# A decoder trunk on one core: one DVE step moved ahead of another at the end of each MLP chunk, and the first tile's loads and the first norm's sums rearranged

## The reference

```python
def rmsnorm(x, g):
    xf = x.astype(jnp.float32)
    y = xf * lax.rsqrt(jnp.mean(xf * xf, axis=-1, keepdims=True) + EPS)
    return (y * g.astype(jnp.float32)).astype(x.dtype)

def mlp_sq_relu(hn, w_up, w_down):
    return jnp.square(jax.nn.relu(hn @ w_up)) @ w_down

for i in range(2):
    h = h + mixer_i(rmsnorm(h, norm_mix[i]))
    h = h + mlp_sq_relu(rmsnorm(h, norm_mlp[i]), w_up[i], w_down[i])
    gate = sigmoid(rmsnorm(h, norm_ple[i]) @ w_ple_gate[i])
    h = h + gate * (p[i] @ w_ple_proj[i])
return rmsnorm(h, norm_final)
```

## Time and profile before

| what | us |
|---|---|
| median of 3 runs | 2712.83 (2710.03 to 2713.29) |
| profiled execution, its own time | 2713.6 |
| span of that execution, first to last instruction | 2712.0 |
| PE busy | 2617.7 (97%) |
| DVE, ACT, POOL busy | 1696.2, 1055.2, 812.5 |
| mean granted TensorE clock | 0.989 of full |

### The profile page before, as it was taken

The page is one execution under the profiler, slowest core; times in us unless marked ns, Lnnn a source line. Parts: engine busy times, 40 slices in busy tenths (PEclk is TensorE's granted clock), DMA queues, the critical chain, the costliest instruction groups (busy, mean ns, idle before and its releaser), DMA issues.

```text
span 2712.0 us, 33195 instructions
## 1 busy us (share of the span) xinstructions
PE 2617.7 (97%) x12228; PEld 2159.2 (80%) x12228; DVE 1696.2 (63%) x2432; ACT 1055.2 (39%) x1758; POOL 812.5 (30%) x687
## 2 busy tenths in 40 slices
PE   7999999799999999999999999989999999999996
PEld 5777888678888888888778888878888888888885
DVE  6766655544667666775664667664566766667555
ACT  5555533433333333334442324353333333333432
POOL 6000000023555555552120000002355554555213
PEclk9999999999999999999999999999999999999998
DMA  3010010031111111111231011013121111111121
GB/s 127 24 32 24 24 32 24 1 117 47 55 55 46 49 50 60 55 49 47 91 103 38 32 32 33 30 40 101 39 62 47 47 55 48 55 55 55 47 78 70
DMA packets 39387, 140.49 MB, mean 52 GB/s; under 512 B 4368, under 2 KB 4384, under 8 KB 39248
## 3 DMA queue, kind: packets, MB, share of 16 engines
q1 hardware_dynamic: 36448, 128.99, 15.4%
q0 software_dynamic: 2224, 7.54, 0.8%
q10 hardware_dynamic: 576, 2.10, 0.2%
HBM read 129.70 MB, written 8.91 MB: 51 GB/s over the span
## 4 chain that ended last, share of the span: by engine, by line
PE 74%; issue 15%; DVE 5%; ACT 4%; DMA 1%; POOL 1%; DVEq 0%; POOLq 0%; SPq 0%; ACTq 0%
PE gemm_ps L480 15%; PE gemm_ps L482 15%; PE gemm_ps L481 15%; PE s_ps L480 7%; PE s_ps L482 7%; PE s_ps L481 7%; PE to_ps L582 1%; DVE wlo L1422 1%; PE to_ps L481 1%; PE to_ps L482 1%; PE to_ps L480 1%; POOL sumsq L884 1%; ACT prob L1090 1%; DVE h L2067 0%; ACT pt_hi L1119 0%
## 5 line engine op out<-in xcount | busy, mean ns | idle before, releaser
L480 PE MATMUL gemm_ps<-b_hi,whi 128*128 128x512 f32 x1280 | 501.4, 392 | 7.8 <-DVE wlo L1422 7.8
L482 PE MATMUL gemm_ps<-b_hi,wlo 128*128 128x512 f32 x1280 | 498.2, 389 | 0.0
L481 PE MATMUL gemm_ps<-b_lo,whi 128*128 128x512 f32 x1280 | 498.2, 389 | 0.0
L480 PE MATMUL gemm_ps<-a_hi,whi 128*128 128x512 f32 x1024 | 428.5, 418 | 20.5 <-DVE a_lo L1431 12.5
L482 PE MATMUL gemm_ps<-a_hi,wlo 128*128 128x512 f32 x1024 | 405.2, 396 | 0.0
L481 PE MATMUL gemm_ps<-a_lo,whi 128*128 128x512 f32 x1024 | 404.5, 395 | 0.0
L1422 DVE TENSOR_TENSOR wlo<-wraw,whi 128x1024 fp32r<-128x1024 f32 x162 | 222.9, 1376 | 136.8 <-ACT whi L1016 136.0
L480 PE MATMUL s_ps<-hid_hi,whi 128*128 128x512 f32 x784 | 305.0, 389 | 0.0
L481 PE MATMUL s_ps<-hid_lo,whi 128*128 128x512 f32 x784 | 305.0, 389 | 0.0
L482 PE MATMUL s_ps<-hid_hi,wlo 128*128 128x512 f32 x784 | 305.0, 389 | 0.0
L480 PEld LDWEIGHTS gemm_ps<-b_hi,whi 128*128 128x128 f32 x1280 | 240.3, 188 | 64.1 <-DVE wlo L1422 13.7
(11 more groups left out here) (261 smaller groups left out, 4481.2 us busy)
## 6 DMA issues: line engine op xcount, KB each, us to landing
wraw<-panels SPq DMA_DIRECT2D x162, 512.0 KB, 3.6
wraw<-pairs SPq DMA_DIRECT2D x56, 512.0 KB, 3.6
h<-x_t SPq DMA_DIRECT2D x12, 512.0 KB, 5.5
h_spill<-h POOLq DMA_DIRECT2D x8, 512.0 KB, 3.1
h<-h_spill SPq DMA_DIRECT2D x8, 512.0 KB, 4.8
out_t<-h SPq DMA_DIRECT2D x8, 512.0 KB, 2.8
h<-x_t ACTq DMA_DIRECT2D x4, 512.0 KB, 10.6
p_raw<-p_t POOLq DMA_DIRECT2D x2, 1024.0 KB, 6.2
```

The source lines that it names most:

```text
L480: nc.tensor.matmul(out, hi_w, hi_x, start=start, stop=False, skip_group_check=True)
L481: nc.tensor.matmul(out, hi_w, lo_x, start=False, stop=False, skip_group_check=True)
L482: return nc.tensor.matmul(out, lo_w, hi_x, start=False, stop=stop, skip_group_check=True)
```

## The change

Three edits. The low part of the next up panel is made after `make_u3` and before the sixth product's read, where it stood after that read. x's tile 0 is loaded in two halves, one as SP's first load and one as ACT's first, both ahead of panel 0; ACT waits for the first half by a semaphore of its own. The first norm's squares are added by DVE, each right after the `a_lo` of its half tile, and POOL's 16 instructions for them are gone, so POOL goes to the masks straight away.

```diff
+        x_first = sem("x_first")
...
+                    sp.dma_start(h[:, 0, half_cols(1)], x_t[0, :, half_cols(1)]).then_inc(x_loaded[0], 16)
                     load_panel(Idx(0))
-                    sp.dma_start(h[:, 0], x_t[0]).then_inc(x_loaded[0], 16)
                     load_panel(Idx(1))
...
-            all_squares(0)
...
+            act.dma_start(h[:, 0, half_cols(0)], x_t[0, :, half_cols(0)]).then_inc(x_first, 16)
             for o in range(1, KT, 2):
                 act.dma_start(h[:, o], x_t[o]).then_inc(x_loaded[o], 16)
...
             for o in range(KT):
-                act.wait_ge(x_loaded[o], 16)
                 for half in range(2):
+                    act.wait_ge(x_first if (o, half) == (0, 0) else x_loaded[o], 16)
                     finish(0, Idx(o), half, a_hi)
...
-                            later = [lambda: None] * 4 + [lambda: w_lo(Idx(n + UPS + 1))] + [lambda: None] * 2
+                            later = [lambda: None] * 3 + [lambda: w_lo(Idx(n + UPS + 1))] + [lambda: None] * 3
...
                     split_lo(0, Idx(o), half, Idx(2 * o + half), a_hi, a_lo)
+                    dve.wait_ge(sq_ready, 2 * o + half + 1)
+                    if o == 0:
+                        V.tensor_copy(sumsq[:, half], zs[:, half]).then_inc(sq_added, 1)
+                    else:
+                        dve.wait_ge(sq_added, 2 * o + half - 1)
+                        V.tensor_tensor(sumsq[:, half], sumsq[:, half], zs[:, half], ALU.add).then_inc(sq_added, 1)
```

## The result

| what | before | after |
|---|---|---|
| median, us | 2712.69 (2710.03 to 2715.31, 6 runs) | 2692.12 (2691.24 to 2693.41, 6 runs) |
| profiled execution, own time | 2713.6 | 2693.33 |
| its span | 2712.0 | 2691.7 |
| granted TensorE clock, mean | 0.989 | 0.989 |

The ratio is 0.9928 (0.9916 to 0.994): 20.6 us faster. The forecast was 2697.3 with a range of 2694.0 to 2702.5. The direction and both mechanisms were right.

What follows compares the result with a forecast made beforehand. PE was taken as the bound, busy 97% of the span, so gains come from its stands or slow matmuls. Boundaries 11.5 plus start 4.8 made 16.3 us off 2713.6, giving 2697.3, range 2694.0 to 2702.5.

Steps and rivals of the forecast that it cites:

- term of 11.5: At 14 up-panel boundaries: the `wlo` moved ahead removes all of PE's 0.82 us each, 11.5 us.
- 4.8: At the start: us gained from halving tile 0's load and adding the squares on DVE, chosen from 3.7 to 5.7.
- So tile 6 ends at 33.7 to 34.7: At the start: PE's end of tile 6, from 14.2 plus 78 matmuls of 17.7 us and slow-pitch losses.
- late end: At the start: slow pitch ends when it did before, 2.8 us lost, tile 6 at 34.7, gain 4.7 us.
- fear of the masks: At the start: POOL's mask selects might hold DVE until 36.4, putting tile 7 at 37.4, a gain of only 3.7 us.
- interpolated 11.8: At the start: panel 1's landing time, interpolated from SP's earlier loads, against 13.8 before.
- early end of my own bounds, 5.7: At the start: 1.8 us lost to slow matmuls, tile 6 at 33.7, tile 7 at 35.4, gain 5.7 us.
- 1.7 us of the norm's sums: At the start, between tiles 6 and 7: the first norm's sums on PE take 1.7 us when nothing is late.
- 14.1 + 7 x 2.6: At the start: DVE handles tiles 1 to 7 from 14.1 at 2.6 us each, ending at 32.4.
- first rival: At the start: shared load engines and slow DVE leave a gain of 0 to 2 us, 2700 to 2702; chance 0.09.
- second rival: At the boundary: POOL takes the port, `wlo` ends at 721.35, 1.4 us lost over 14, total 2710; chance 0.05.
- third rival: POOL takes the port throughout: `wlo` ends at 721.7, 7 us lost, nothing won at the start, 2720.6; chance 0.02.

Runs made afterwards that it cites:

- masks_late: Changed kernel with POOL's mask building held back until DVE's sixteen additions of the first norm are done: 2692.85 us.
- start_only: Kernel before plus only the halved tile 0 loads and the first norm's sums on DVE, without the moved `wlo`: 2704.81 us against 2711.55.
- pool_ahead: Changed kernel with two memsets of dead tiles on DVE ahead of each boundary's `wlo`: 2703.23 us, 11.1 more than the changed kernel.
- boundary_only: Kernel before plus only the `wlo` moved ahead of the sixth product's read: 2699.61 us against 2711.55.
- pool_first: Changed kernel with one short memset of a dead tile on DVE ahead of each boundary's `wlo`: 2692.8 us.

## Why the prediction was right in kind and short in size

**Edit 1: right.** The waits went, the `wlo` stands right behind `make_u3` with 1.22 us and 0.7 us to spare, and POOL pays, as predicted. The term of 11.5 was a little small. From the pair's last matmul to the panel's tenth took 3.14 us before and 2.27 now, so a boundary gave 0.87 and not 0.82: a few matmuls behind a stall run at 0.23 to 0.24 as well, which I had not counted. 14 x 0.87 = 12.2, and 11.9 and 12.1 were measured alone.

**Edits 2 and 3: the term that was mis-sized.** I took 4.8; the trace shows 41.1 - 34.3 = 6.8 at tile 7. The step that failed is "So tile 6 ends at 33.7 to 34.7"; it ended at 32.63. On top of that I took 4.8 out of the 4.7 to 5.7 that follow, its late end, for fear of the masks. The 6.8 is no outlier: in the ten traces that have both edits of the start and no other change of it, the third panel's first matmul comes at 37.63 to 38.91, and at 45.01 to 45.19 in the three that have neither, so 6.1 to 7.6 us are won. (I count `masks_late` among the ten.) Two parts make up the missing 2.0:

- Panel 1 landed at 11.1, not at the interpolated 11.8, and its first matmul stood at 13.52, not 14.2. That is 0.7.
- The slow pitch. By my sum from 14.2 the choice of 4.8 holds 2.7 us of it behind that point; the trace has 32.63 - 13.52 - 78 x 0.2275 = 1.4. That is 1.3. (The early end of my own bounds, 5.7, holds 1.8.) For the late end I had let the slow pitch end at the same time as before, near 20; it ended at 16.25. Counting PE's rows of 0.6 us and more ahead of 30 us, the four executions without edit 2's loads have 14, 13, 19 and 19 of them, the twelve with them (and without added matmuls) 6 to 12, 8.8 on average. At 0.43 - 0.23 = 0.20 each, the difference of 7 is 1.5 us; between the two profiled executions, 14 and 12, it is less. What differs in the rows is that in the four PE stands 1.5 to 2.0 us in front of `to_ps`, and in the twelve 0.5 at most. So the edit seems to have won twice, the stand and the pitch behind it. That the stand is the cause of the slow matmuls was not tried by itself.

The 1.7 us of the norm's sums came as predicted. DVE was never what PE waited for behind tile 0, and it ended at 32.4, as I had written (14.1 + 7 x 2.6 is 32.3), but by luck: it took up tile 1 at 13.4 and not at 14.1, and needed 1.35 us for a half on average and not 1.3, as its `a_lo` beside the masks went up to 0.93. The first rival (the start gives little) fell by `start_only`.

**The rest.** Against the profiled executions' own times the forecast is 20.3 - 16.3 = 4.0 short: 2.0 at the start, 0.7 at the boundaries, 0.7 in PE's waits for the load of p (2.7 before, 2.0 after), and 0.6 that I cannot place. The waits for p came to 1.3 to 2.7 us in the other traces with no order in it, so that 0.7 is chance. The median after lies a further 1.2 below its own profiled execution. (Counted by medians, the gain is 20.6 and not 16.3, and the sum started from 2713.6, 0.9 above the median before.) With a term of 6.8 and 12.2 the sum would have been 2694.6 from the profiled execution, inside the range and still 2.5 above the median. So the low end of the range was too near as well: it held 0.9 us for the start, where that alone was off by 2.0, a little for the boundary, and 1.7 for the runs' spread.

**Slower, or no change:** `pool_ahead` shows the second rival at work (the `wlo` ends 3.16 behind `make_u3`'s start, the rival had 721.35 - 718.06 = 3.29). In the changed kernel it did not occur: DVE's row starts 0.16 ahead of POOL's, and even with a memset that put it 0.11 behind DVE went first. The rivals read the rows a little too dear. The `wlo` of 1.61 in the earlier trace rows starts at 721.87 while POOL's addition runs until 720.19 + 2.21 = 722.40, and ends 1.08 behind that, as it does with 1.09 in `pool_ahead`. So the 1.61 already holds the wait, and the third rival, which sets it behind POOL's end (720.13 + 1.61), counts the wait twice; behind POOL the `wlo` would have ended near 721.2, as late as in the kernel before and not later.

## What to carry to other kernels

Where an engine issues in order and another waits for one of its results, look which instruction nobody waits for stands in front of it, and whether the cause of that result is already there; then look at the place one further ahead, since there the same step cost 10 of the 12 us that it had won. At a program's start, a late operand can cost more than the stand: here executions with a stand of 1.5 to 2.0 us had 13 to 19 slow matmuls and those without it 6 to 12, though that the one causes the other is not shown. Gains under 2 us ahead of a long stage with its own spread are to be read at their place in the trace, since the median may not show them.

## What was not expected of the hardware

- The number of slow matmuls at the start differs between executions of the same kernel: 12 and 6 in the changed kernel, 13 and 19 in `boundary_only`, 7 and 11 in `start_only`. 24 small matmuls ahead of them took it to 0 once, and in the other execution PE fell back to the slow pitch after three matmuls, with a granted clock of 0.50 from 11.5 to 18.0 us.
- A VectorE instruction with two SBUF inputs whose row starts 0.11 us behind a GpSimd one still went first (`pool_first`); 0.66 us behind, it was held for 0.5 us of its 1.73. In both cases the held row starts on time and is longer by the wait.
